# Gate projections beside attention: seven Strassen products for eight, their weights combined and split by other engines

## The chip, the cores and the metric

The kernel runs on one core of a Trainium2 chip. The metric is the device time of one execution in microseconds (us); three executions of the kernel before gave 3804.57, 3805.02 and 3805.33 us, so the median is 3805.02.

## The reference, cut to what matters

The program computes two transformer-like blocks one after the other, all in fp32 on 1024 tokens with 1024 features. The change touches the second block. It begins with one wide projection, whose last 4096 columns are four gates of 1024 features, and four mixers, of which the attention is one:

```python
h = rmsnorm_2(x, g_mix)
u = h @ w_in                                    # 28 blocks of 128 columns, then 32 blocks of gates
c_q, c_kv, k_r, u_pool, z, xbc, dt, lru_g, lru_x, gates = split(u)
y_a = mla_mixer(c_q, c_kv, k_r, ...)            # causal attention: 8 heads, 1024 queries
y_b, y_c, y_d = pool_mixer(...), ssd_mixer(...), rglru_mixer(...)
gates = sigmoid(gates.reshape(b, s, 4, 1024))
merged = gates[0] * (y_a @ w_branch[0]) + ... + gates[3] * (y_d @ w_branch[3])
```

## The kernel before, in words

Names in rows: `m_` are the tiles of this projection, `at_` those of attention, `sd_` those of the state-space mixer before it, `t_` and `b_` those of later stages (`b_high`, `b_rest` and `b2_high` also hold h here). PE is TensorE, ACT ScalarE, DVE VectorE, POOL GpSimd, SP SyncE. `ACTq` and `SPq` rows are DMA issues by that engine.

An fp32 product is made as three matmuls (`product3`, L98 to L102): every operand is split in a rounded high part and the low rest, and high by high (L100), high weight by low input (L101) and low weight by high input (L102) are summed in PSUM. Each of these takes 128 contracted rows, 128 weight columns and 512 tokens.

`Projection` makes the wide projection in units of 128 columns. The weights of a unit are 128x1024 (8 blocks of contraction): SP loads them (L2641, 512 KB), POOL rounds them (L2652) and forms the rest (L2654), PE multiplies them with h, 8 blocks by 3 matmuls for each of the two halves of 512 tokens, ACT copies each half out of PSUM (`take`, L2701), SP stores (L2707). Units 0 to 27 run beside the earlier mixers. The 32 gate units run inside `Attention`: they are what PE does while it waits for the softmax, in pieces of 24 matmuls before the loop (4, 3, 1 and 1 pieces) and in half pieces of 12 matmuls in it. The gates are 32 units x 2 halves x 24 = 1536 matmuls.

The order on each engine is written out by hand. `Attention` first reads its projections (ACT issues the loads, L3325 to L3331), takes the squares for two norms (L3341), makes values, queries and keys, and then loops over 64 steps n = 8h + b: head h, block b of 128 queries. In a step PE turns the probabilities of n (L3292), makes the scores of n+1 (L3254; at b = 7 the queries of the next head, L3235), does its half pieces (two for even b, one for odd b), and then multiplies probabilities and values of n (L3302). After b = 7 it does two half pieces more, then the first scores of the next head. DVE takes the maximum of the scores of n+1 (`greatest`, L3443 to L3450), and later scales the result of n (L3472). ACT copies the turned probabilities of n out of PSUM (L3384), then takes the exponential of n+1 (`weigh`, L3354, after the maximum), then copies gate halves (L2701). POOL only splits gate weights in this time, and SP only loads and stores for the gates. Engines wait for each other by semaphores and run their own list strictly in order.

## Time and profile before

| | |
|---|---|
| median of 3 runs | 3805.02 us |
| profiled execution, own time | 3803.0 us |
| its span | 3801.3 us |
| PE busy | 3474.2 us (91%) |
| DVE, ACT, POOL busy | 2420.9, 1581.9, 1122.8 us |
| mean granted TensorE clock | 0.957 |
| matmuls of the projection and gates (L100 m_b) | 960, 404.7 us |

A busy time is summed over one engine's instructions; the engines run beside each other. Idle time of an engine is given with what released it. Times within the span (2225.00, say) are us from its start.

### The profile page before, as it was taken

To read this page: it belongs to the slowest core of one execution; us is meant where nothing else is said; L and a number is where in the kernel's file an instruction comes from. 1 tells how busy PE (TensorE), PEld (TensorE's weight loads), DVE (VectorE), ACT (ScalarE), POOL (GpSimd) and SP (SyncE) were. 2 spreads that over 40 slices of the span, in tenths; PEclk is the share of its full clock that TensorE was granted. 3 is DMA by queue.
4 is the path that set the end of the run, shared out by engine and by line. 5 is a ranking of instruction groups with operands and counts; after the bars stand their busy time and mean duration, and the time that the engine had idled before them with its cause. 6 is when DMAs were issued, how large, how long until landed. Compare 5 with 4: busy or idle time off the path is not lost. (4 is left out here: it accounts for less than half of the span.)

```text
span 3801.3 us, 44335 instructions
## 1 busy us (share of the span) xinstructions
PE 3474.2 (91%) x16324; PEld 2772.5 (73%) x16324; DVE 2420.9 (64%) x2818; ACT 1581.9 (42%) x2197; POOL 1122.8 (30%) x673
## 2 busy tenths in 40 slices
PE   6899998596999999879989899999899889999997
PEld 3678777465888888756777667777677778878876
DVE  5569557747888888867655322222246488877778
ACT  4322234445777777735222222222232342234444
POOL 1232220145111111143321212222143455545543
PEclk9899999797999999989999999999999999999999
DMA  5312246647999999854421311111253524478854
GB/s 190 112 50 82 105 144 215 223 153 280 406 402 407 403 407 400 353 214 141 147 92 56 128 47 67 59 67 64 79 193 128 194 97 153 152 285 275 267 167 138
DMA packets 224984, 716.69 MB, mean 189 GB/s; under 512 B 26816, under 2 KB 61457, under 8 KB 208689
## 3 DMA queue, kind: packets, MB, share of 16 engines
q1 hardware_dynamic: 184000, 620.37, 45.0%
q10 hardware_dynamic: 31056, 64.28, 4.5%
q0 software_dynamic: 9760, 29.80, 2.0%
q8 instruction: 106, 1.74, 0.2%
q14 instruction: 62, 0.50, 0.0%
HBM read 573.47 MB, written 140.89 MB: 188 GB/s over the span
## 5 line engine op out<-in xcount | busy, mean ns | idle before, releaser
L100 PE MATMUL m_b<-b_high,m_high 128*128 128x512 f32 x960 | 404.7, 422 | 12.4 <-POOL m_low L2654 6.6
L102 PE MATMUL m_b<-b_high,m_low 128*128 128x512 f32 x960 | 377.3, 393 | 0.0
L101 PE MATMUL m_b<-b_rest,m_high 128*128 128x512 f32 x960 | 376.8, 393 | 0.0
L2652 POOL TENSOR_TENSOR m_high<-m_raw,m_one 128x1024 fp32r<-128x1024 f32 x60 | 119.2, 1986 | 761.3 <-PE m_b L102 684.0
L3948 POOL TENSOR_TENSOR t_wl<-t_buf,t_wh 128x512 fp32r<-128x512 f32 x136 | 195.2, 1441 | 240.6 <-ACT t_wh L4079 240.5
L100 PE MATMUL zs_z<-zs_hs,zs_high 128*128 128x512 f32 (+1 forms) x584 | 226.1, 387 | 8.5 <-DVE zs_hs L310 8.0
L2701 ACT ACTIVATE m_ob<-m_b 128x512 f32<-128x512 f32 x120 | 71.1, 596 | 376.3 <-PE m_b L102 341.1
L100 PEld LDWEIGHTS m_b<-b_high,m_high 128*128 128x128 f32 x960 | 182.7, 190 | 60.6 <-issue 12.4
L100 PE MATMUL t_b<-b_high,t_wh 128*128 128x512 f32 x544 | 215.4, 396 | 9.5 <-POOL t_wl L3948 9.5
L101 PE MATMUL zs_z<-zs_hs,zs_high 128*128 128x512 f32 (+1 forms) x584 | 218.7, 375 | 0.0
L102 PE MATMUL zs_z<-zs_hs,zs_low 128*128 128x512 f32 (+1 forms) x584 | 218.6, 374 | 0.0
L101 PEld LDWEIGHTS m_b<-b_rest,m_high 128*128 128x128 f32 x960 | 182.9, 190 | 45.9 <-issue 8.4
L101 PE MATMUL t_b<-b_rest,t_wh 128*128 128x512 f32 x544 | 213.7, 393 | 0.0
L102 PE MATMUL t_b<-b_high,t_wl 128*128 128x512 f32 x544 | 213.4, 392 | 0.0
L102 PEld LDWEIGHTS m_b<-b_high,m_low 128*128 128x128 f32 x960 | 182.0, 190 | 40.0
L2278 DVE TENSOR_TENSOR ex_wlo<-moe_raw,ex_who 128x2048 fp32r<-128x2048 f32 x78 | 178.7, 2292 | 50.4 <-ACT ex_who L2228 49.5
L2278 DVE TENSOR_TENSOR moe_mixl<-moe_late_rows,moe_mixh 128x2048 fp32r<-128x2048 f32 x78 | 178.8, 2293 | 42.4 <-ACT moe_mixh L2228 42.4
L4079 ACT ACTIVATE t_wh<-t_buf 128x512 fp32r<-128x512 f32 x136 | 85.8, 631 | 261.7 <-PE t_b L102 77.6
L2278 DVE TENSOR_TENSOR moe_mixl<-moe_raw,moe_mixh 128x2048 fp32r<-128x2048 f32 x80 | 182.5, 2283 | 5.3 <-PEq L48 5.3
L428 POOL TENSOR_TENSOR zs_high<-zs_raw,zs_one 128x1024 fp32r<-128x1024 f32 x29 | 59.0, 2035 | 411.8 <-PE zs_z L102 406.4
L3472 DVE TENSOR_SCALAR at_o<-m_b,at_sm 128x64 f32<-128x64 f32 x64 | 18.2, 284 | 230.2 <-PE m_b L3302 203.0
L2228 ACT ACTIVATE ex_who<-moe_raw 128x2048 fp32r<-128x2048 f32 x78 | 149.1, 1913 | 23.4 <-DMA moe_raw<-in_expert_w 18.2
(710 smaller groups left out, 9454.8 us busy)
## 6 DMA issues: line engine op xcount, KB each, us to landing
moe_raw<-in_expert_w SPq DMA_DIRECT2D x79, 2048.0 KB, 10.1
moe_late_rows<-in_expert_w SPq DMA_DIRECT2D x39, 2048.0 KB, 10.4
t_raw<-in_w_ff SPq DMA_DIRECT2D x192, 256.0 KB, 3.6
m_raw<-in_w_ug SPq DMA_DIRECT2D x60, 512.0 KB, 4.5
t_buf<-hid SPq DMA_DIRECT2D x112, 256.0 KB, 4.4
hid<-t_x SPq DMA_DIRECT2D x96, 256.0 KB, 2.3
yrows<-ex_y ACTq DMA_DIRECT2D x38, 512.0 KB, 11.4
gates<-m_ob SPq DMA_DIRECT2D x32, 512.0 KB, 2.9
```

The costliest lines, as they stand in the source:

```text
L100: nc.tensor.matmul(out, w[0], x[0], start=first, stop=False)
L101: nc.tensor.matmul(out, w[0], x[1], start=False, stop=False)
L102: return nc.tensor.matmul(out, w[1], x[0], start=False, stop=last)
L428: g.tensor_tensor(self.high[j][:], self.raw[j][:], self.one[:].broadcast_to([P, D]), ALU.mult).then_inc(self.rounded, 1)
L2228: S.activation(half(wh[u], x_), half(raw[slot], x_), ACT.Copy).then_inc(rounded, 1)
L2278: V.tensor_tensor(half(wl[u], x_), half(raw[slot], x_), half(wh[u], x_).bitcast(F32), ALU.subtract).then_inc(left, 1)
L2652: g.tensor_tensor(W.high[j][:], W.raw[j][:], W.one[:].broadcast_to([P, D]), ALU.mult).then_inc(W.rounded, 1)
L2701: self.nc.scalar.activation(self.ob[n % 2][:, c * BANK:(c + 1) * BANK], self.banks[m % len(self.banks)][:], ACT.Copy).then_inc(self.taken, 1)
L3472: V.tensor_scalar(self.o[p % 2][:, b, h % 2 * VH:(h % 2 + 1) * VH], ps[4][:, n % 2 * P:n % 2 * P + VH], sm[:, 1:2], None, ALU.mult).then_i ...
L3948: G.tensor_tensor(self.wl[:, f % 4], self.source(f), self.wh[:, f % 4].bitcast(F32), ALU.subtract).then_inc(self.split, 1)
L4079: S.activation(self.wh[:, f % 4], self.source(f), ACT.Copy).then_inc(self.rounded, 1)
```

## The change

The gates become a product of a 2 by 2 block matrix: the 1024 columns of contraction in two halves of 512, the 1024 tokens in two halves, and the 32 gate units as 16 pairs (units g and g + 16). For each pair Strassen's scheme (in the Winograd form) makes seven products of combined inputs instead of eight, each of 4 blocks of contraction by 3 matmuls. So there are 16 x 7 = 112 products f of 12 matmuls, 1344 in all. They run in seven phases of 16: ONE (f 0 to 15), TWO, THREE, SIX, SEVEN, FOUR, FIVE. Pieces before the loop become 8, 6, 2 and 2 products (216 matmuls, as many as the 4, 3, 1 and 1 pieces were); a step of the loop has one product, two at b = 4 and 6, and two more at a head's end: 12 for a head, where there were 14 half pieces.

What is new per product: SP loads 128x512 blocks of the weights (L2852) into seven places; where a product wants a sum of blocks, POOL makes it (`sum`, L2898); ACT rounds it (`high`, L2925, for up to three products ahead, LEAD); POOL forms the rest (`split`, L2911) in the order sum of product f+1, then the rest of f. One sum of three blocks per pair (`KEPT_SUM`, two POOL additions) is formed after product 13 + 3g//2, written to DRAM (`gate_sum`, L2816) and loaded again as one term of phases THREE and SIX. The products of ONE are copied out by ACT (L2960); the later ones are added by DVE (L2972) to partial results that SP stores and reads again (L2879, L2866); in phases SIX and FIVE DVE adds twice. The combined inputs of h for SIX, SEVEN, FOUR and FIVE are formed in place by DVE in 72 additions spread over the steps (`transform`, L2985 to L2997), and rounded by ACT (`round`, L3008). The combination of the seven products replaces no other work of the kernel; `take` for the gates is gone.

The diff, cut to its core; tables of places, the reads of partial results and the steps of `transform` are left out:

```diff
-        self.nc, self.R, self.h, self.total, self.banks = nc, R, h, 2 * N_UG, banks
-        self.W = Weights(nc, s, A["w_ug"], D, N_UG)
+        self.nc, self.R, self.h, self.total, self.banks = nc, R, h, 2 * N_U, banks
+        self.W = Weights(nc, s, A["w_ug"], D, N_U)
...
+class Gates:
+    PAIRS = 16
+    ONE, TWO, THREE, SIX, SEVEN, FOUR, FIVE = range(7)
+    KEPT = None
+    WEIGHTS = (((0, 0, 1),), ((0, 1, 1),), ((0, 1, 1), (KEPT, 0, -1)), ((KEPT, 0, 1),), ((0, 0, 1), (1, 0, -1)), ((1, 1, 1),), ((1, 0, 1), (1, 1, 1)))
+    KEPT_SUM = ((1, 0, 1), (1, 1, 1), (0, 0, -1))
...
+    RING, AHEAD, READ_AHEAD, LEAD = 4, 3, 2, 3
...
+        self.raw = [W.raw[0][:, lo], W.raw[0][:, hi], W.raw[1][:, lo], W.raw[1][:, hi], room[0], F.ob[1][:, lo], F.ob[1][:, hi]]
...
+        keep_after = {13 + 3 * g // 2: g for g in range(self.PAIRS)}
+        self.jobs = []
+        for f in range(self.total):
+            self.jobs.append(("product", f))
+            if f in keep_after:
...
+        self.sums_to, n = {}, 0
+        order = [("product", 0)]
+        for job in self.jobs:
+            order += [job] if job[0] == "keep" else [("product", job[1] + 1)] if job[1] + 1 < self.total else []
...
+    def keep_to(self, sp, g):
+        while self.kept_to <= g:
+            job = ("keep", self.kept_to)
+            sp.wait_ge(self.summed, self.sums_to[job])
+            sp.dma_start(self.R["gate_sum"][job[1]], self.raw[self.slot(job, 0)]).then_inc(self.kept, 16)
+            self.kept_to += 1
...
+    def weights(self, sp, job):
+        for i, (r, c, sign) in enumerate(self.terms[job]):
+            n = self.first_load[job] + i
+            slot = n % len(self.raw)
+            if n >= len(self.raw):
+                before, part = self.owner[n - len(self.raw)]
+                if part:
+                    sp.wait_ge(self.summed, self.sums_to[before] - len(self.terms[before]) + 1 + part)
+                elif before[0] == "keep":
+                    self.keep_to(sp, before[1])
+                    sp.wait_ge(self.kept, 16 * (before[1] + 1))
+                else:
+                    sp.wait_ge(self.split, before[1] + 1)
...
+            if r is self.KEPT:
+                g = job[1] % self.PAIRS
+                self.keep_to(sp, g)
+                sp.wait_ge(self.kept, 16 * (g + 1))
+                source = self.R["gate_sum"][g]
+            else:
+                source = self.A["w_ug"][N_U + job[1] % self.PAIRS + self.PAIRS * r][:, c * BANK:(c + 1) * BANK]
+            sp.dma_start(self.raw[slot], source).then_inc(self.w_in[slot], 16)
...
+    def store(self, sp, f):
+        x, g = divmod(f, self.PAIRS)
+        if x == self.ONE:
+            sp.wait_ge(self.copied, f + 1)
+        else:
+            sp.wait_ge(self.added, f - self.PAIRS + 1)
...
+    def step(self, sp, f):
+        self.weights_to(sp, f + self.AHEAD)
+        self.read(sp, f + self.READ_AHEAD)
+        self.store(sp, f)
...
+    def sum(self, pool, job):
+        terms = self.terms[job]
+        raw = self.raw[self.slot(job, 0)]
+        for i in range(1, len(terms)):
+            if i == 1:
+                self.landed(pool, job, 0)
+            self.landed(pool, job, i)
+            self.nc.gpsimd.tensor_tensor(raw, raw, self.raw[self.slot(job, i)], ALU.add if terms[i][2] > 0 else ALU.subtract).then_inc(self.summed, 1)
+            pool.wait_ge(self.summed, self.sums_to[job] - len(terms) + 1 + i)
+    def split_all(self, pool):
+        self.sum(pool, ("product", 0))
+        for job in self.jobs:
+            if job[0] == "keep":
+                self.sum(pool, job)
+                continue
+            f = job[1]
+            if f + 1 < self.total:
+                self.sum(pool, ("product", f + 1))
+            pool.wait_ge(self.high_made, f + 1)
+            self.nc.gpsimd.tensor_tensor(self.wl[f % self.RING], self.raw[self.slot(job, 0)], self.wh[f % self.RING].bitcast(F32), ALU.subtract).then_inc(self.split, 1)
+    def high(self, act, count):
+        for f in range(self.highs, min(count, self.total)):
+            job = ("product", f)
+            if len(self.terms[job]) > 1:
+                act.wait_ge(self.summed, self.sums_to[job])
+            else:
+                self.landed(act, job, 0)
+            if f >= self.RING:
+                act.wait_ge(self.used, f - self.RING + 1)
+            else:
+                act.wait_ge(self.F.W.used[f // 2], N_U // 2)
+            self.nc.scalar.activation(self.wh[f % self.RING], self.raw[self.slot(job, 0)], ACT.Copy).then_inc(self.high_made, 1)
+            self.highs += 1
...
+    def multiply(self, pe, count):
+        for f in range(self.made, min(self.made + count, self.total)):
+            x, j = f // self.PAIRS, f % self.RING
+            pe.wait_ge(self.split, f + 1)
...
+            for k in range(4):
+                for n in made:
+                    pe.wait_ge(self.t_low, n + k + 1)
+                part = slice(k * P, (k + 1) * P)
+                mm = product3(self.nc, self.bank(f), (self.wh[j][:, part], self.wl[j][:, part]), (high[k], low[k]), k == 0, k == 3)
+            mm.then_inc(self.used, 1)
+            self.made += 1
+    def copy(self, act, count):
...
+            act.wait_ge(self.used, f + 1)
+            self.nc.scalar.activation(self.part[slot], self.bank(f), ACT.Copy).then_inc(self.copied, 1)
+            self.out += 1
+            self.high(act, f + 1 + self.LEAD)
+    def add(self, dve, count):
+        for f in range(self.out, min(self.out + count, self.total)):
+            x = f // self.PAIRS
+            for slot, _, n in self.uses[f]:
+                dve.wait_ge(self.part_in[slot], 16 * (n + 1))
+            dve.wait_ge(self.used, f + 1)
+            for slot, _, _ in self.uses[f]:
+                ins = self.nc.vector.tensor_tensor(self.part[slot], self.part[slot], self.bank(f), ALU.subtract if x == self.FOUR else ALU.add)
+            ins.then_inc(self.added, 1)
+            self.out += 1
...
-        self.fills = [2 - b % 2 for b in range(self.QB)]
+        self.fills = [1 + (b in (4, 6)) for b in range(self.QB)]
...
     def tensor(self, pe):
-        F.multiply(pe, 4)
+        G.multiply(pe, 8)
...
-        F.multiply(pe, 3)
+        G.multiply(pe, 6)
...
-            F.halves(pe, self.fills[b])
+            G.multiply(pe, self.fills[b])
...
-                F.halves(pe, 2)
+                G.multiply(pe, 2)
...
     def scalar(self, act):
-        F.take(act, 4)
+        G.high(act, G.LEAD)
+        G.copy(act, 8)
...
+        made = 18
...
-            take(self.fills[b])
+            G.high(act, made + G.LEAD)
+            G.round(act, n)
+            made += self.fills[b] + 2 * last
             if last:
                 if h % 2:
                     pair(h // 2)
-                take(2)
...
     def vector(self, dve):
...
+            G.add(dve, self.fills[b])
+            G.transform(dve, n)
             dve.wait_ge(self.summed, n + 1)
...
+            if last:
+                G.add(dve, 2)
+        G.add(dve, G.total)
...
+                for f in range(G.total):
+                    G.step(sp, f)
+                G.over(sp)
...
-                for n in range(2, N_UG):
+                for n in range(2, N_U):
                     F.halve(pool_, n)
+                G.split_all(pool_)
```

Three places show how the instructions move. First ACT at the start of attention, with the issue of the last store of the state-space mixer (`sd_xo`). Before:

```order
L2701 ACTIVATE m_ob1<-m_b6 128x512
L3184 DMA y<-sd_xo 128x4x1024
L3331 DMA at_cq<-u 128x3x1024
...
L3331 DMA at_pT1<-in_w_uv 128x1024
L3325 DMA at_wq0<-in_w_uq 128x384
L3327 DMA at_wk0<-in_w_uk 128x256
L2701 ACTIVATE m_ob0<-m_b7 128x512
L2701 ACTIVATE m_ob0<-m_b5 128x512
L2701 ACTIVATE m_ob1<-m_b6 128x512
L2701 ACTIVATE m_ob1<-m_b7 128x512
L3341 ACTIVATE at_pT0<-at_cq 128x512 x3
```

The same place of the changed kernel:

```order
L2701 ACTIVATE m_ob1<-m_b6 128x512
L3482 DMA y<-sd_xo 128x4x1024
L3629 DMA at_cq<-u 128x3x1024
...
L3629 DMA at_pT1<-in_w_uv 128x1024
L3623 DMA at_wq0<-in_w_uq 128x384
L3625 DMA at_wk0<-in_w_uk 128x256
L2925 ACTIVATE m_high0<-m_raw0 128x512 x2
L2925 ACTIVATE m_high1<-m_raw1 128x512
L2960 ACTIVATE m_ob0<-m_b7 128x512
L2925 ACTIVATE m_high1<-m_raw1 128x512
L2960 ACTIVATE m_ob0<-m_b5 128x512
```

The rounding of the first gate weights, which POOL did by itself before, now stands on ACT behind the store and eight DMA issues.

Second, ACT at the turn from head 0 to head 1, the last copies of step 7 first (at_pr holds the exponentials, at_pT the turned probabilities). Before:

```order
L3384 ACTIVATE at_pT1<-m_b2 128x512
L3384 ACTIVATE at_pT1<-m_b3 128x512
L2701 ACTIVATE m_ob0<-m_b7 128x512
...
L2701 ACTIVATE m_ob1<-m_b5 128x512
L3354 ACTIVATE at_pr0,at_sm0<-m_b0,at_mx0 128x128
L3325 DMA at_wq1<-in_w_uq 128x384
L3384 ACTIVATE at_pT0<-m_b2 128x128
L3354 ACTIVATE at_pr1,at_sm1<-m_b0,at_mx1 128x256
L2701 ACTIVATE m_ob1<-m_b6 128x512
```

The same place of the changed kernel; the three rounds after the second exponential are those of products 30, 31 and 32:

```order
L3676 ACTIVATE at_pT1<-m_b2 128x512
L3676 ACTIVATE at_pT1<-m_b3 128x512
L2925 ACTIVATE m_high0<-m_raw1 128x512
L2925 ACTIVATE m_high0<-m_ob1 128x512
L3008 ACTIVATE b2_high<-at_t 128x512
L3653 ACTIVATE at_pr0,at_sm0<-m_b0,at_mx0 128x128
...
L3676 ACTIVATE at_pT0<-m_b2 128x128
L3653 ACTIVATE at_pr1,at_sm1<-m_b0,at_mx1 128x256
L2925 ACTIVATE m_high1<-m_raw1 128x512
L2925 ACTIVATE m_high1<-at_groom0 128x512
L2925 ACTIVATE m_high0<-m_raw0 128x512
```

In the changed kernel product 30, which PE has next after the scores of block 1, is rounded behind the exponential of these scores; before, ACT had nothing there that the pieces of PE wait for.

Third, SP where the gates begin; from there to the end of attention it goes on in this alternation. Before:

```order
L2707 DMA u<-m_ob0 128x1024
L2641 DMA m_raw1<-in_w_ug 128x1024
L2707 DMA u<-m_ob1 128x1024
L2641 DMA m_raw0<-in_w_ug 128x1024
L2707 DMA gates<-m_ob0 128x1024
L2641 DMA m_raw1<-in_w_ug 128x1024
L2707 DMA gates<-m_ob1 128x1024
```

In the changed kernel SP has this where kept sums and products of two terms meet (head 1, products 32 and 33; the weight and partial loads and the stores of results alternate with writes of kept sums):

```order
L2852 DMA m_ob1<-in_w_ug 128x512 x2
L2816 DMA gate_sum<-m_raw0 128x512
L2852 DMA m_raw0<-in_w_ug 128x512 x2
L2852 DMA m_raw1<-gate_sum 128x512
L2866 DMA at_kr<-gate_part 128x512
L2879 DMA gates<-at_groom1 128x512
L2852 DMA m_raw1<-in_w_ug 128x512
L2852 DMA at_groom0<-in_w_ug 128x512
L2816 DMA gate_sum<-m_ob1 128x512
L2852 DMA m_ob1<-in_w_ug 128x512 x2
L2852 DMA m_raw0<-gate_sum 128x512
```

And POOL there, from the sum of product 32 to the rest of product 32:

```order
L2898 TENSOR_TENSOR m_raw0<-m_raw0,m_raw1 128x512
L2911 TENSOR_TENSOR m_low1<-at_groom0,m_high1 128x512
L2898 TENSOR_TENSOR m_ob1<-m_ob1 128x512
L2898 TENSOR_TENSOR m_ob1<-m_ob1,m_raw0 128x512 x2
L2911 TENSOR_TENSOR m_low0<-m_raw0,m_high0 128x512
```

The places of the seven blocks come round after two or three products, so that a load of SP stands behind the write of a kept sum, and the rest of a product stands on POOL behind the sum of the next one and a kept sum.

## Rows read from the trace of the kernel before

**Rows 1.** Busy time, stretch by stretch: attention's loop.
```profile
core 0: us, PE busy (x) PEld busy (x) DVE busy (x) ACT busy (x) POOL busy (x), PEclk, DMA share, GB/s
2225.00:2745.00 520.00, 505.13 (x2501) 396.17 (x2499) 129.76 (x435) 138.70 (x346) 110.94 (x52) 1.00 0.18 61
```

**Rows 2.** Waits in the same stretch: engine, line, releaser; us, times, longest.
```profile
POOL m_high L2652 <- PE m_b L102: 379.1, 26, 21.2
ACT m_ob L2701 <- PE m_b L102: 150.0, 39, 7.3
PE m_b L3292 <- ACT at_pr L3354: 9.8, 7, 1.4
```

**Rows 3.** Timeline of PE and ACT, start of attention: start, us, instruction, idle before.
```profile
2124.83 0.39 PE L100 MATMUL m_b<-b_high,m_high 128*128 128x512 f32 x1
...
2125.04 0.38 ACTq L3184 DMA_DIRECT2D y<-sd_xo  x1
...
2134.14 0.37 ACTq L3331 DMA_DIRECT2D at_cq<-u  x1
...
2138.38 1.09 ACT L2701 ACTIVATE m_ob<-m_b 128x512 f32<-128x512 f32 x2 [12.76 <-issue]
...
2146.36 0.39 PE L102 MATMUL m_b<-b_high,m_low 128*128 128x512 f32 x1
...
2148.48 1.15 ACT L3341 ACTIVATE at_pT<-at_cq 128x512 f32<-128x512 f32 x2 [1.09 <-DMA at_pT<-in_w_uv]
```

**Rows 4.** The page's costliest groups: ACT rounding 128x512 in a later stage.
```profile
L4079 ACT ACTIVATE t_wh<-t_buf 128x512 fp32r<-128x512 f32 x136 | 85.8, 631 | 261.7 <-PE t_b L102 77.6
```

**Rows 5.** POOL forming rests, by tile: ns least/median/most, first and last start.
```profile
L3948 POOL TENSOR_TENSOR t_wl<-t_raw,t_wh x90: 1268/1295/1770, 3032.3 to 3634.3; 128x512 fp32r<-128x512 f32 x90
L2654 POOL TENSOR_TENSOR m_low<-m_raw,m_high x60: 2338/2390/3442, 1641.1 to 2703.0; 128x1024 fp32r<-128x1024 f32 x60
```

**Rows 6.** Timeline of PE where it had waited, and a stretch there (columns as rows 1).
```profile
2220.17 0.33 PE L3292 MATMUL m_b<-all_ident,at_pr 128*128 128x128 f32 x1 [2.23 <-ACT at_pr L3354]
...
2220.58 0.97 PE L100 MATMUL m_b<-b_high,m_high 128*128 128x512 f32 x1
...
2227.64 0.39 PE L102 MATMUL m_b<-b_high,m_low 128*128 128x512 f32 x1
```
```profile
2221.00:2223.00 2.00, 2.00 (x6) 1.58 (x5) 0.95 (x4) 0.57 (x2) 0.00 (x0) 0.50 0.00 0
```

**Rows 7.** Timeline at the start of a head.
```profile
2355.18 0.33 PE L3292 MATMUL m_b<-all_ident,at_pr 128*128 128x128 f32 x1 [1.40 <-ACT at_pr L3354]
2355.35 0.60 PE L3254 MATMUL m_b<-at_k,at_q 128*128 128x256 f32 x2
...
2355.59 0.58 PE L100 MATMUL m_b<-b_high,m_high 128*128 128x512 f32 x1
2355.98 0.30 DVE L3443 TENSOR_TENSOR m_b<-m_b,all_cutq 128x128 f32<-128x128 f32 x1 [1.35 <-PE m_b L3254]
...
2356.77 0.15 DVE L3450 TENSOR_SCALAR at_mx<-at_mx 128x1 f32<-128x1 f32 x1
...
2356.96 0.48 ACT L3354 ACTIVATE at_pr<-m_b,at_mx 128x256 f32<-128x256 f32 x1 [1.14 <-DVE at_mx L3450]
...
2357.34 0.19 ACT L3354 ACTIVATION_READ_ACCUMULATOR at_pr<-m_b,at_mx 128x1 f32 x1
...
2361.04 0.39 PE L102 MATMUL m_b<-b_high,m_low 128*128 128x512 f32 x1
```

**Rows 8.** VectorE's groups by line and shape: busy, mean ns, idle before.
```profile
L4360 DVE TENSOR_TENSOR b_rest<-t_buf,b_high 128x512 fp32r<-128x512 f32 x64 | 77.7, 1226 | 23.8 <-ACT b_high L4122 23.1
L4369 DVE TENSOR_TENSOR t_x<-t_x,t_b 128x512 f32<-128x512 f32 x48 | 32.9, 685 | 6.5 <-PE t_b L102 4.3
```

**Rows 9.** The page's DMA issues: KB each, median us from issue to landing.
```profile
t_raw<-in_w_ff SPq DMA_DIRECT2D x192, 256.0 KB, 3.6
...
hid<-t_x SPq DMA_DIRECT2D x96, 256.0 KB, 2.3
```

**Rows 10.** Timeline of SP's issue, and of PE four steps on in the same head.
```profile
2362.01 0.69 PE L100 MATMUL m_b<-b_high,m_high 128*128 128x512 f32 x1
...
2362.45 0.43 SPq L2641 DMA_DIRECT2D m_raw<-in_w_ug  x1
...
2388.12 0.69 PE L100 MATMUL m_b<-b_high,m_high 128*128 128x512 f32 x1
```

More of the change, by code:

```diff
@@ L3219, in tensor @@
     def tensor(self, pe):
-        mm_, ps, C, turn, F = self.nc.tensor.matmul, self.ps, self.C, self.nc.tensor.transpose, self.F
-        F.multiply(pe, 4)
+        mm_, ps, C, turn, G = self.nc.tensor.matmul, self.ps, self.C, self.nc.tensor.transpose, self.gates
+        G.multiply(pe, 8)
         for c in range(2):
@@ L3344, in scalar @@
             S.activation(self.rs[w][:], self.rs[w][:], ACT.Sqrt).then_inc(self.rooted, 1)
-        F.take(act, 3)
+        G.copy(act, 6)
         for c in range(self.QB):
@@ L3365, in pair @@
             act.dma_start(self.R["y"][p], self.yT[:]).then_inc(self.stored, 16)
-        F.take(act, 2)
+        G.copy(act, 2)
         weigh(0)
         weights(1)
-        begun, made = 0, F.moved
-        def take(parts):
-            nonlocal begun
-            begun += parts
-            F.take(act, made + begun // 2 - F.moved)
+        made = 18
         for n in range(MH * self.QB):
@@ L3476, in vector @@
                 greatest(n + 1)
+            if last:
+                G.add(dve, 2)
+        G.add(dve, G.total)
     def over(self, eng):
@@ L3497, in mixers @@
             att = Attention(nc, s, q, A, R, F, banks, C, rope, (ssd,))
+            G = att.gates = Gates(nc, s, q, A, R, F, att, ssd)
         with nc.Block() as block:
@@ L3509, in _ @@
                 lru.constants(sp)
-                for n in range(N_UG):
+                for n in range(N_U):
                     if n >= 2:
@@ L3519, in _ @@
                     ssd.load(sp, n)
-                for n in range(N_UG - 2, N_UG):
+                    if n == N_U - 2:
+                        G.weights_to(sp, G.AHEAD - 1)
+                for n in range(N_U - 2, N_U):
                     F.landed(sp, n)
+                for f in range(G.total):
+                    G.step(sp, f)
+                G.over(sp)
                 att.over(sp)
@@ L3547, in _ @@
                 att.scalar(act)
-                F.take(act, N_UG * 2)
             @block.vector
```

162 lines of the change are left out of this document (151 added, 11 removed).

## The prediction

> **What bounds the kernel now.** I read first the stretch by stretch view of attention's loop, then the waits of that stretch, then the timelines of its start and of one head. In the loop PE is busy for 505.13 of 520.00 us at a granted clock of 1.00, while DVE, ACT and POOL have 129.76, 138.70 and 110.94 us [rows 1]. The waits say the same: POOL waits 379.1 us and ACT 150.0 us for PE's matmuls, and PE's only wait of size is 9.8 us, seven times at a head's start, for the first exponential of a head [rows 2]. So in this stretch every matmul left out is time gained, and every wait that PE is given is time lost. What hides the gates' other work is that it is done a whole unit ahead of PE.
>
> **A. The matmuls that go.** 1536 become 1344, so 192 go. From 2124.83 to 2146.36 PE starts 96 in a row, 95 distances in 21.53 us, 0.2266 us each [rows 3]. 192 x 0.2266 = 43.5 us gained, all on the path, since PE has nothing else to wait for there. The matmuls before the loop stay 216, so this is all gained in the loop.
>
> **B. The start of attention.** Before, the weights of the first gate unit are split by POOL, which has nothing else to do, and PE goes on at 2124.83. After, the first rounding is on ACT, behind the store of the state-space output and eight DMA issues. ACT issues that store at 2125.04, issues the next DMA only when it has landed, at 2134.14, and is free at 2138.38 [rows 3]. Then come one rounding, for which the nearest row is 0.631 us [rows 4], and one rest, 1.295 us [rows 5], with the hops between: PE starts product 0 at about 2140.4, 15.6 us late. Before, ACT was held just as long, but only copies of PSUM stood there, and three banks took PE's pieces meanwhile. The squares, which start at 2148.48, are the next thing on the path and move with PE, since they stand behind the copy of product 7 now, and ACT rounds product 10 first (0.6 and a copy, 1.5 in all). PE is also idle long enough to lose its clock. After an idle time of 2.23 us the granted clock was 0.50 in the next 2 us, which is the lower level, 1.2 GHz, and the 24 matmuls behind it took 7.06 us from the first start to the last end's start [rows 6], against 5.45 us for the same 24 in the middle of the loop, from 2355.59 to 2361.04 [rows 7]: 1.6 us. B is 15.6 + 1.6 + 1.5 = 19 us, between 13 (the time that ACT is held, 2125.04 to 2138.38) and 22.
>
> **C. The start of heads 1 to 7.** ACT rounds for three products ahead, but counts the two products of a head's end only after them, so at b = 7 it has rounded just to the end of the head. The first product of the new head is rounded behind the exponential of block 1. PE reaches that product right after the scores of block 1, and waits for the maximum (2355.98 to 2356.92, 0.94 us), the exponential with its read-out (2356.96 to 2357.53, 0.57) [rows 7], the rounding (0.63) and the rest (1.30): 3.4, with hops 3.7 us. In the row the pieces simply start at 2355.59, while DVE and ACT do this. Nothing else covers it: PE's next work, probabilities by values, stands behind the product. Does the clock fall for 3.7 us? The rows show both: 2.23 us of idle lost it and 1.6 us [rows 6], and the usual 1.40 us at a head's start did not, as the clock over the loop is 1.00 [rows 1, 7]. 3.7 lies beyond the one that lost it, and I take the loss. So 7 x (3.7 + 1.6) = 37.1, and at the two heads where DVE's double additions (0.685 each [rows 8], two more of them) stand ahead of the maximum 2 x 1.4 = 2.8: 39.9 us. The bounds are 7 x 3.4 = 24, without a loss of clock, and 47, with one more addition at each head.
>
> The Trainium skill, page "TensorE: Matmul & The Clock Gate", section "HAM oscillation — how this bites in real kernels", has a rule that speaks against the change: work on TensorE that is short between two waits starts cold after each wait, so the price is paid at every one of them. By it the sum has C at 39.9; by the 1.40 us row alone C would be 28.7 and the time 3842. The trace agrees with the rule for 2.23 us of idle and not for 1.40.
>
> **D. Kept sums among products of two terms (products 31 to 36).** Seven places hold the weight blocks. From product 31 to 36 each product wants two blocks, and four kept sums want three each, so a block is loaded when the job two back lets go of it, and that job is often a kept sum that must be added, written and read first. Per step of the long kind: two POOL sums of 128x512 (half of a 128x1024 operation of 2.39 us, 1.2 each [rows 5]) 2.4; write of the kept sum 2.3 [rows 9]; two or three issues on SP's queue, of which one is 0.43 [rows 10], 1.1; landing of 256 KB 3.6 [rows 9]; sum 1.2 and rest 1.3 [rows 5]: 11.7 us with one rest at the end. A short step, with the kept sum already out, has issue, landing, sum and rest, 6.5 us. I read the order of the queues as long, short, short, long, short: 43 us. PE goes through the five products in 23.4 us: four steps from 2362.01 to 2388.12 [rows 10] are 26.1 us, less one half piece of 2.7. The chain is 19.5 us longer. To that I add 3 us since the rest of product 31 stands on POOL behind the sum of 32, whose loads stand on SP behind a store of a result that DVE adds only after the new head's first maximum, and two cold starts, 3.2. D is 26 us. This is the least sure term: if the loads run ahead by three products as they do elsewhere it is 0, and if every step is long (5 x 11.7 - 23.4 and the rest) 45.
>
> **E. The start of the loop.** The loads of products 20 and 21 stand on SP behind the store of product 16, and DVE adds that only after the first maximum; ACT blocks in `high` meanwhile. PE's lead there is two products, so a few us come out: 4, between 0 and 8.
>
> **F. VectorE.** DVE takes on 96 products of one or two additions (128 x 0.685 = 88 us [rows 8]) and 72 transforms, for which the nearest row is a subtraction of two 128x512 SBUF operands, 1.226 us [rows 8]: 88 us. With its 130 it has some 306 of about 480 us. The additions stand behind exponential and sum in each step, with a product (2.7 us) of cover before the maximum of the step after next; where a transform piece and two products fall together the maximum is late. 3 us, between 0 and 10. ACT takes on some 107 roundings of 0.63 and gives up 55 copies; POOL has 94 rests and 80 sums of about 1.25 us, 218 us in place of 111, and DMA some 496 transfers of 256 KB, about 260 GB/s in place of 61: all have room on average [rows 1], and I cost them at nothing beyond B to E. What covers them is PE's 5.1 us per product (480 by 94); if that cover were gone, POOL would cost 2.3 us a product.
>
> **Sum.** -43.5 + 19 + 39.9 + 26 + 4 + 3 = +48.4 us on the profiled execution's 3803.0, so 3851.4. The median of the runs lies 2.0 above that execution (3805.02), so I forecast 3853 us. By the lower bounds it is -43.5 + 13 + 24 = -6.5 us, 3798; by the upper ones -43.5 + 22 + 47 + 45 + 8 + 10 = +88.5, 3893.
>
> **The rivals.**
> 1. *The chain of kept sums never reaches PE* (not slower). The loads of 31 to 36 run far enough ahead, since POOL and DMA idle on average, and the clock survives waits of 3.7 us. Then D, E and F are 0, C is its lower 24, B 19: -0.5 us, 3804. For it: 379 us of idle POOL [rows 2]. Against it: the seven places and SP's strict order leave no way to run ahead. It decides once PE's lead over the rests stays above one product through product 36. A step on is its other half: if in addition PE's start is covered, because B's 13 us of waiting were ACT's alone and something of attention could move up, it is -43.5 + 24 = -19.5, 3785. Against that: PE's list has nothing between the first product and the squares.
> The Trainium skill has a rule that backs this rival, on the page "DMA: Bandwidth & Descriptors", section "Rules for kernel authors": issued early and waited for late, a transfer's fixed cost lies beside the computing. By that rule D would be 0. No row of this trace shows a load held by a reused place as short as these.
> 2. *DVE and POOL hold each other up* (slower still). 72 transforms and 174 operations of POOL work on SBUF in the same time. If each transform waited for one operation of POOL, 72 x 1.3 = 94 us would come on DVE, of which about half is beyond its free time in the steps where they fall: +45, 3898. For it: rests on POOL take up to 1.77 us where the median is 1.295 [rows 5]. Against it: that the median is so near the least, 1.268, with DVE at work in the same stretch.
> The Trainium skill, page "SBUF — State Buffer", section "SBUF: two separate sides", says that VectorE and GpSimd share a pair of ports and that an operation with two SBUF inputs locks the other out for its whole length. The medians do not show it as a rule for every operation.
> 3. *PE is not the bound*, so that the matmuls left out bring nothing. 505 of 520 us busy [rows 1] excludes it.
>
> **How the numbers follow.** A run can tell 0.2% from no change, 7.6 us here: below 3797.4 is faster, above 3812.6 slower. The forecast, slower by 0.2% to 2.3%, has 0.72; rival 2 0.06; rival 1 0.12 without and 0.10 with its second half. So faster 0.10, same 0.12, slower 0.78. The range is 3797 to 3893, the two sums of bounds rounded out, with 0.16 outside.
>
> **What would show it.** A: 192 fewer matmuls of L100 to L102 on m_b. B: PE idle for 15 us before the first product of attention, released by POOL's rest, and ACT's first rounding right behind its DMA issues. C: seven waits of PE for POOL's rest of over 3 us at the starts of heads 1 to 7, and clock 0.50 behind them. D: waits of PE for the rest of products 32 to 36 in head 1 of together some 20 us, with POOL waiting for DMA. F: waits of PE for exponentials longer than 1.4 us. The prediction is wrong if PE has no such wait at the heads, if those in D sum to under 5 us, or if waits for DVE or for partial results, which I cost at nothing, are the largest.

## The result, and the profile after

The changed kernel took 3876.03 us in the median of four runs, 1.0192 of the kernel before (interval 1.018 to 1.0205), some 71 us more. The forecast was 3853 with a range to 3893, so sign and main mechanism held and the size came out a third too small. The profiled execution has a span of 3875.2 us, 73.9 more than before, and the whole difference lies in the stretch of attention, from the first gate product that PE could take (2124.83 before, 2126.28 after) to the end of attention's last matmul (2740.36 and 2815.68): 615.5 us became 689.4. The stretch, and below it the loop, of before and then of after (columns as in [rows 1]):

```profile
2124.83:2740.36 615.53, 596.40 (x2809) 455.64 (x2807) 163.72 (x466) 159.16 (x380) 132.35 (x62) 0.99 0.20 69
2220.17:2740.36 520.19, 509.96 (x2514) 400.04 (x2514) 130.71 (x439) 138.46 (x347) 110.94 (x52) 1.00 0.18 61
```
```profile
2126.28:2815.68 689.40, 586.91 (x2616) 438.52 (x2616) 316.57 (x666) 200.95 (x460) 254.08 (x192) 0.93 0.59 202
2241.15:2815.68 574.53, 497.19 (x2322) 380.96 (x2322) 279.60 (x639) 164.83 (x401) 216.51 (x165) 0.93 0.62 208
```

The second numbers carry the account. PE has 2809 - 2616 = 193 operations fewer on record (192 by the program), worth 43.5 us at the forecast's price, but its busy time fell by only 9.5 us: what was left ran 34.0 us longer, at a mean granted clock of 0.93 in place of 0.99. And PE's idle time rose from 19.1 to 102.5 us, 83.4 more. -9.5 + 83.4 = 73.9. What PE waited for in the stretch (us, times, longest):

```profile
PE m_b L100 <- POOL m_low L2911: 69.9, 16, 14.5
PE m_b L3590 <- ACT at_pr L3653: 16.4, 16, 1.4
PE m_b L3539 <- DVE at_ckv L3703: 6.0, 1, 6.0
PE m_b L3600 <- ACT at_pT L3676: 5.6, 2, 4.9
```

Before, there was no wait of the first kind, and the second was this over the whole loop ([rows 2] begins after the first of the eight):

```profile
PE m_b L3292 <- ACT at_pr L3354: 12.0, 8, 2.2
```

So the 16.4 us are eight more waits, none longer than 1.4. The largest of the first kind, in the changed kernel, in order of time (start, us of the matmul, and in brackets the wait before it): one before the loop, five in head 1, and one at the start of each later head, those of heads 4 and 5 left out here:

```profile
2140.74 0.80 PE L100 MATMUL m_b<-b_high,m_high 128*128 128x512 f32 x1 [14.46 <-POOL m_low L2911]
...
2321.53 0.80 PE L100 MATMUL m_b<-b_high,m_high 128*128 128x512 f32 x1 [5.15 <-POOL m_low L2911]
2331.82 0.50 PE L100 MATMUL m_b<-b_high,m_high 128*128 128x512 f32 x1 [4.33 <-POOL m_low L2911]
2344.92 0.79 PE L100 MATMUL m_b<-b_high,m_high 128*128 128x512 f32 x1 [6.90 <-POOL m_low L2911]
2360.99 0.80 PE L100 MATMUL m_b<-b_high,m_high 128*128 128x512 f32 x1 [3.33 <-POOL m_low L2911]
2373.97 0.80 PE L100 MATMUL m_b<-b_high,m_high 128*128 128x512 f32 x1 [7.50 <-POOL m_low L2911]
2421.55 0.80 PE L100 MATMUL m_b<-b_high,m_high 128*128 128x512 f32 x1 [3.70 <-POOL m_low L2911]
2490.16 0.79 PE L100 MATMUL m_b<-b_high,m_high 128*128 128x512 f32 x1 [4.49 <-POOL m_low L2911]
...
2698.20 0.80 PE L100 MATMUL m_b<-b_high,m_high 128*128 128x512 f32 x1 [3.50 <-POOL m_low L2911]
2763.45 0.79 PE L100 MATMUL m_b<-b_high,m_high 128*128 128x512 f32 x1 [4.55 <-POOL m_low L2911]
```

The start of head 6 shows the chain of term C, and answers to [rows 7]: maximum, exponential, then the rounding, then the rest, and PE's first product of the head only behind it.

```profile
2694.10 0.60 PE L3552 MATMUL m_b<-at_k,at_q 128*128 128x256 f32 x2
...
2695.53 0.15 DVE L3743 TENSOR_SCALAR at_mx<-at_mx 128x1 f32<-128x1 f32 x1
...
2695.72 0.47 ACT L3653 ACTIVATE at_pr<-m_b,at_mx 128x256 f32<-128x256 f32 x1 [1.14 <-DVE at_mx L3743]
...
2696.18 1.14 ACT L2925 ACTIVATE m_high<-m_raw 128x512 fp32r<-128x512 f32 x2
2696.88 2.49 POOL L2911 TENSOR_TENSOR m_low<-m_raw,m_high 128x512 fp32r<-128x512 f32 x2 [20.27 <-ACT m_high L2925]
```

POOL's idle time of 20.27 us before its rest, and ACT's rounding without a wait of its own right behind the exponential, say that nothing but ACT's place in line was late.

Head by head, from the first turn of a head to that of the next (the last to the end of the stretch), in us; "start" is what lies ahead of head 0:

| | start | 0 | 1 | 2 | 3 | 4 | 5 | 6 | 7 |
|---|---|---|---|---|---|---|---|---|---|
| before | 95.3 | 66.2 | 68.8 | 64.6 | 68.8 | 64.5 | 68.8 | 64.6 | 53.8 |
| before less 24 matmuls (5.4) | 95.3 | 60.7 | 63.4 | 59.1 | 63.4 | 59.1 | 63.4 | 59.1 | 48.4 |
| after | 114.9 | 74.5 | 101.5 | 67.8 | 72.8 | 67.4 | 68.8 | 64.2 | 57.6 |
| lost against line 2 | 19.5 | 13.7 | 38.1 | 8.7 | 9.4 | 8.2 | 5.4 | 5.0 | 9.2 |

### The profile page after: what moved, and what is told of

Same layout as the page of the kernel before. It is cut to its first block and busy times, and to the rows that moved or that the text cites. A ratio compares the mean times of both kernels' runs of the same rounds, so it can differ in the third digit from the quotient of the medians.

```text
span 3875.2 us, 45336 instructions
## 1 busy us (share of the span) xinstructions
PE 3468.5 (90%) x16132; PEld 2758.7 (71%) x16132; DVE 2572.0 (66%) x3018; ACT 1623.8 (42%) x2277; POOL 1235.2 (32%) x801
## 5 line engine op out<-in xcount | busy, mean ns | idle before, releaser
L100 PE MATMUL m_b<-b_high,m_high 128*128 128x512 f32 x896 | 390.0, 435 | 82.3 <-POOL m_low L2911 69.9
L102 PE MATMUL m_b<-b_high,m_low 128*128 128x512 f32 x896 | 362.0, 404 | 0.0
L101 PE MATMUL m_b<-b_rest,m_high 128*128 128x512 f32 x896 | 361.7, 404 | 0.0
L2278 DVE TENSOR_TENSOR ex_wlo<-moe_raw,ex_who 128x2048 fp32r<-128x2048 f32 x78 | 178.7, 2292 | 50.4 <-ACT ex_who L2228 49.7
L2228 ACT ACTIVATE moe_mixh<-moe_raw 128x2048 fp32r<-128x2048 f32 x76 | 145.7, 1918 | 25.4 <-PE ex_pu L102 24.0
L2652 POOL TENSOR_TENSOR m_high<-m_raw,m_one 128x1024 fp32r<-128x1024 f32 x28 | 58.7, 2098 | 289.7 <-PE m_b L102 221.6
L4253 POOL TENSOR_TENSOR t_wl<-t_raw,t_wh 128x512 fp32r<-128x512 f32 x90 | 121.8, 1362 | 86.1 <-ACT t_wh L4384 85.9
```

The lines of the kernel that those rows point to most:

```text
L100: nc.tensor.matmul(out, w[0], x[0], start=first, stop=False)
L101: nc.tensor.matmul(out, w[0], x[1], start=False, stop=False)
L102: return nc.tensor.matmul(out, w[1], x[0], start=False, stop=last)
L2228: S.activation(half(wh[u], x_), half(raw[slot], x_), ACT.Copy).then_inc(rounded, 1)
L2278: V.tensor_tensor(half(wl[u], x_), half(raw[slot], x_), half(wh[u], x_).bitcast(F32), ALU.subtract).then_inc(left, 1)
L2652: g.tensor_tensor(W.high[j][:], W.raw[j][:], W.one[:].broadcast_to([P, D]), ALU.mult).then_inc(W.rounded, 1)
```

## The experiments

Ratios are to the kernel before, measured beside each experiment, with their 95% interval; a stretch is that of attention in the profiled execution, as above (689.4 us in the changed kernel).

**1. The first product of a head rounded before the head's first exponential.**

```diff
                 if h + 1 < MH:
+                    G.high(act, made + 1)
                     weigh(n + 1)
```

> The changed kernel, but at a head's end ACT rounds the first product of the next head before the exponential of that head, not behind the second one. My theory (PE waits at the starts of heads 1 to 7 because that rounding stands behind the exponential): the seven waits for POOL's rest, 28.5 us together in the changed kernel's trace, go, and the clock that PE loses behind each (about 1.5 us) with them; head 1 gives some of it back since the kept sums are late there anyway. So 3876 less 30 to 39: about 3842. Rival (the rounding is only one of two late things, the loads or the sums behind it are as late): the waits stay with another releaser, and the time is over 3862.

Measured: 1.0164 (1.0147 to 1.018), 3861.39 us, some 11 us less than the changed kernel's ratio makes, with runs from 3852.95 to 3869.17; the profiled one is the fastest of them, with a stretch of 670.3, 19.1 less. By the ratio, a third of my 30 to 39 us came, and the heads of the fastest run say why. Heads 3, 5 and 6 went from 72.8, 68.8 and 64.2 to 66.3, 63.4 and 59.1, that is 6.5, 5.4 and 5.1 less, and their clock was 1.00. Heads 2, 4 and 7 stayed at 68.0, 66.9 and 56.4: there the wait moved to the second product (4.24, 4.84 and 2.84 us). Head 1 gave 2.1 us, the kept sums holding it as before. POOL makes the sum of the next product ahead of the rest of this one, so a second product waits where the third is a sum of two blocks. That is so in heads 2, 4 and 7, in phases THREE, SEVEN and FIVE; head 5 begins with the last two sums of SEVEN, but its third product, like those of heads 3 and 6, wants one block. So the theory holds where the third product wants one block, and the rival where it wants two. In head 2 of this run the store of a result stands on SP (2410.97) behind DVE's additions, which come after the new head's first maximum; only then SP issues the load of a kept sum for product 44, and POOL's sum waits 9.54 us for it, ahead of the rest of 43:

```profile
2409.81 0.15 DVE L3744 TENSOR_SCALAR at_mx<-at_mx 128x1 f32<-128x1 f32 x1
...
2410.26 0.69 DVE L2972 TENSOR_TENSOR m_sin<-m_sin,m_b 128x512 f32<-128x512 f32 x1 [0.30 <-issue]
...
2410.97 0.32 SPq L2879 DMA_DIRECT2D gate_part<-m_sin  x1
...
2412.04 0.40 SPq L2852 DMA_DIRECT2D m_raw<-gate_sum  x1
...
2416.62 1.26 POOL L2898 TENSOR_TENSOR m_ob<-m_ob,m_raw 128x512 f32<-128x512 f32 x1 [9.54 <-DMA m_raw<-gate_sum]
```

**2. The first products rounded before ACT waits for the store.**

```diff
         S, ps, F, G = self.nc.scalar, self.ps, self.F, self.gates
+        G.high(act, G.LEAD)
+        G.copy(act, 1)
         for e in self.earlier:
             e.over(act)
...
-        G.high(act, G.LEAD)
-        G.copy(act, 8)
+        G.copy(act, 7)
```

> The changed kernel, but ACT rounds the first three products and copies the first result out before it waits for the state-space store and issues attention's loads. My theory (PE's 14.5 us of waiting before product 0 come from that place on ACT): PE works through products 0 to 3 in that time and waits some 2 us before product 4, so 10 to 13 us less, about 3864. Rival (the next stage waits for loads that land as late as before, so that PE waits the same before the squares): under 4 us less, over 3872.

Measured: 1.0197 (1.018 to 1.0214), 3875.90 us, no change. The rival held, as to its kind: PE's wait of 14.46 us became waits of 2.55, 1.87, 1.85 and 3.79, and the first sums of squares came only 1 us earlier. The next thing was the loads: that of product 5 stands on SP behind the store of product 1, which waits for ACT's copy, which stands behind the eight DMA issues. ACT then waited 7.28 us for it:

```profile
2138.45 0.60 ACT L2960 ACTIVATE m_ob<-m_b 128x512 f32<-128x512 f32 x1 [3.75 <-issue]
...
2139.07 0.33 SPq L2879 DMA_DIRECT2D gate_part<-m_ob  x1
2139.45 0.43 SPq L2852 DMA_DIRECT2D m_ob<-in_w_ug  x1
...
2147.33 0.63 ACT L2925 ACTIVATE m_high<-m_ob 128x512 fp32r<-128x512 f32 x1 [7.28 <-DMA m_ob<-in_w_ug]
```

**3. No kept sums.**

```diff
-        keep_after = {13 + 3 * g // 2: g for g in range(self.PAIRS)}
+        keep_after = {}
...
-    WEIGHTS = (..., ((0, 1, 1), (KEPT, 0, -1)), ((KEPT, 0, 1),), ...
+    WEIGHTS = (..., ((0, 1, 1), (0, 0, -1)), ((0, 0, 1),), ...
```

> The changed kernel without the kept sums: no three loads, two additions, write and reload for a pair; phases THREE and SIX take one plain block in the place of the kept sum, so two of the three terms of that sum are left out of the result. Loads, sums of two terms, partial results and transforms stay. My theory (the waits of PE for the rests of products 31 to 36, 22 us and some 8 us of clock, and those of head 0, some 10 us, come from the kept sums' loads and writes in the seven places): 30 to 42 us less, about 3840, and no wait over 2 us in heads 0 and 1 but that at the head's start. Rival (products of two terms alone, or the partial results, hold the chain): the waits of head 1 stay at over half, and the time is over 3860.

Measured: 1.007 (1.0053 to 1.0087), 3829.69 us, some 46 less, more than the 30 to 42 of my theory; stretch 644.3. Head 0 went from 74.5 to 59.8, head 1 from 101.5 to 71.6, the others by less than 2 us. All that head 0 had lost is the kept sums' (59.8 against 60.7 in line 2 of the table), and 29.9 us of head 1. The waits at the heads' starts stayed, 3.50 in head 1 to 4.56 in head 7.

**4. The kernel before with fewer matmuls.**

```diff
+        cut = part is not None and ms[0] % 5 == 0
-        for k in range(KD) if part is None else range(part * KD // 2, (part + 1) * KD // 2):
+        for k in (... as before ...) if not cut else (part * (KD - 1),):
```

> The kernel before, with 198 of the gates' 1536 matmuls left out inside the loop (18 of 24 in every fifth piece, 11 pieces; their products are left out of the result); loads, splits, copies and stores stay. My theory (PE is the bound in the loop, 0.2266 us a matmul): 44.9 us less, about 3760. Rival (other engines or the softmax chain come out as soon as PE has less to do): half of that or less, over 3782.

Measured: 0.9906 (0.9889 to 0.9922), 3766.55 us, 35 us less, 0.18 a matmul where I had 0.2266. PE is the bound, but not alone: where a cut piece stood, the exponential was late. These waits rose from the eight of 12.0 us to

```profile
PE m_b L3293 <- ACT at_pr L3355: 19.2, 14, 2.6
```

This experiment cut 9 of the 12 matmuls of a half piece, often both halves of a piece in one step, more unevenly than the change does; heads 5 and 6 of experiment 1 show the full 5.4 us.

**5. The kept sums at other places.**

```diff
-        keep_after = {13 + 3 * g // 2: g for g in range(self.PAIRS)}
+        keep_after = {11: (0, 1, 2), 17: tuple(range(3, 9)), **{19 + 2 * i: (9 + i,) for i in range(7)}}
...
-        self.weights_to(sp, f + self.AHEAD)
+        self.weights_to(sp, f + (5 if f in (7, 13) else self.AHEAD))
```

> The changed kernel with the kept sums at other places: three after product 11 and six after product 17, where PE does norms, keys and values, and the other seven after products 19, 21 to 31, one for two products, none after 31; SP's loads run two products further ahead at these two places. Leaving the sums out altogether took 45 us off the stretch. My theory (the cost lies in where the sums stand: four of them among the products of two terms, and 1.5 products apart in heads 0 and 1): 25 to 40 us less than the changed kernel, about 3843, and no wait over 2 us between the starts of heads 1 and 2 but the one at the start. Rival (seven places are too few for the sums wherever they stand, so the waits only move into the time before the loop): under 12 us less, over 3862.

Measured: 1.0177 (1.016 to 1.0194), 3873.05 us, some 6 us less by the ratio, within the two intervals. The rival held: head 1 got shorter, from 101.5 to 77.5, but in its place came a wait of 6.42 before product 12 and one of 19.92 at the first turn of head 0. The sums put after product 17 could not begin there, since ACT rounds 17 only after the values; they ran from 2232.91 on, and ACT stood 25.89 us in the rounding of a product whose block is loaded behind theirs, with the first exponential in its queue.

**6. The second with the loads of products 0 to 6 ahead of the first store.**

```diff
+                G.weights_to(sp, 6)
                 for f in range(G.total):
                     G.step(sp, f)
```

> The changed kernel with the early rounding of the second experiment, and SP issues the loads of products 0 to 6 before its first store of a result. The early rounding alone gave nothing, as products 5 and 6 then waited for their loads, which stand on SP behind a store that waits for ACT's copy. My theory (two holds in a row: ACT's place, and SP's order): 8 to 12 us less than the changed kernel, about 3866. Rival (the third thing, ACT's eight DMA issues, which hold the copies and the roundings of the next products till 2138, is as late): under 4 us less, over 3871.

Measured: 1.0182 (1.0165 to 1.0199), 3872.84 us, some 3 us less, within the two intervals: by the time, the rival's outcome. In the profiled run, the fastest of the four, the stretch is 683.6, 5.8 less, and the wait of 3.79 before product 5 is gone, so the loads were one hold. Two more are seen in its trace, and no run takes them apart: product 4, whose rounding stands right behind ACT's eight issues (PE waits 2.54), and ACT's waits for a store to land (4.11) and for the next loads (2.49, 1.92 and 2.16) ahead of the squares, for which PE waits 4.05.

**7. All repairs at once,** with one of DVE's two additions at a head's end ahead of the first maximum:

```diff
+                G.add(dve, 1)
                 greatest(n + 1)
+                G.add(dve, 1)
-            if last:
+            elif last:
                 G.add(dve, 2)
```

> The changed kernel with the repairs of the head's start, of the attention's start and of the kept sums together, and one of the two additions at a head's end ahead of the first maximum. Sum of the parts by my theory: start of heads 19 as measured plus what the kept sums hid of it (10), kept sums 30, start 10: 69 us less than the changed kernel's 3876, about 3807, level with the kernel before. Rival (the products of two terms hold the heads' starts and the chain through the loads as well): 25 us or more stay, about 3832.

Measured: 1.0046 (1.0029 to 1.0063), 3824.16 us, between the two. The new wait of experiment 5 is in it (20.26 us before head 0), and still the heads 2 to 6 came to 61.7, 66.0, 60.2, 63.4 and 59.4: the earlier addition, with the earlier rounding, took the wait from the heads with two blocks too. Neither the rounding alone (experiment 1) nor the other places alone (experiment 5: 68.2 and 68.1) shortened heads 2 and 4; the earlier addition alone was not run.

**8. No transforms.**

```diff
-        for x in range(16):
+        for x in range(0):
...
-            made = [4 * i for i, t in enumerate(self.T) if t[0] == x and f % self.PAIRS == 0]
+            made = []
```

> The changed kernel with the 72 additions on h and their 16 roundings left out (phases SIX to FIVE multiply with plain blocks of h, so the results are not the gates). My theory (DVE has room; they cost PE some late maxima only): 3 to 8 us less, about 3870. Rival (DVE and POOL hold each other up on SBUF, or DVE's list is what makes maxima late at most steps): over 20 us less, under 3856.

Measured: 1.0164 (1.0147 to 1.0181), some 10 us less, stretch 680.3: 9.1 less, a little over what I expected of my theory and far from the rival. PE's waits for exponentials fell from 16.4 us (16) to 11.4 (9), which is the late maxima; the other 4 us were not followed.

**9 and 10. The repairs with the kept sums placed by what experiment 5 showed.**

```diff
-        keep_after = {11: (0, 1, 2), 17: tuple(range(3, 9)), **{19 + 2 * i: (9 + i,) for i in range(7)}}
+        keep_after = {10: (0, 1), 16: tuple(range(2, 8)), **{18 + 7 * i // 4: (8 + i,) for i in range(8)}}       # 9
+        keep_after = {10: (0,), 16: tuple(range(1, 6)), **{17 + 3 * i // 2: (6 + i,) for i in range(10)}}        # 10
```

> All repairs of the seventh experiment, with the kept sums placed by what its trace showed: its sums after product 17 began only at 2225, since the rest of 17 stands behind ACT's rounding of 17, which comes after the values, and so held the first exponential 20 us; those after 11 held product 11 for 6 us. Now two after product 10, six after 16 (whose rest is formed before the values), and eight from 18 to 30. My theory (the wait before the loop is the sums' chain holding ACT's rounding of products 20 and 21): 20 to 28 us less than the seventh's 3824, about 3799, within 0.2% of the kernel before. Rival (the sums cost the same wherever they stand, as their loads come through the same seven places): under 8 us less, over 3816.

> The same with one kept sum after product 10, five after 16 and ten from 17 to 30, 1.5 products apart as in the changed kernel. Theory: fewer sums before the loop, so no wait there, but the waits of head 0 (4.9 us, and some of 1 to 2) stay: within 5 us of the run before it, about 3801. Rival (as there): over 3816.

In both, SP's loads run one product further ahead at the two places where experiments 5 and 7 had two.

Measured: experiment 9 0.9988 (0.9979 to 0.9998), 3799.82 us, as forecast: it beats the kernel before by 0.12%, with an interval that ends just short of none. Experiment 10, 1.0017 (1.0008 to 1.0026), 3809.56, missed: I had it within 5 us of experiment 9, and with ten sums in the loop in place of eight it took some 10 us more. Its profile, of one of its slowest runs (3816.40), has a wait of 8.87 us before the second product of head 1, where experiment 9 has 5.02. Experiments 3, 5, 9 and 10 together say that the price of a kept sum is mostly that of its place. In the profile of experiment 9, the stretch and PE's first waits in it:

```profile
2124.20:2735.58 611.38, 566.48 (x2617) 423.24 (x2616) 323.01 (x666) 200.44 (x460) 254.63 (x192) 0.98 0.68 228
```
```profile
PE m_b L100 <- POOL m_low L2910: 19.1, 11, 5.0
PE m_b L3589 <- ACT at_pr L3653: 16.6, 16, 1.4
```

611.4 us against 615.5 before, with the changed kernel's waits for exponentials and 19.1 us in place of 69.9 for rests. The start takes 105.7 us, still 10 more than before, and head 1 keeps that one wait. Against line 2 of the table the stretch still loses 39 us: 10.4 at the start, 9.1 and 7.2 in heads 0 and 1, 5.4 in head 7 and 7 in the others together. So nearly all that the missing matmuls are worth is still spent.

## Why the prediction was right, and where its sizes were off

**What bounds, and A.** Right. With the wait at its start gone, heads 5 and 6 of experiment 9 take 63.4 and 59.3 us, where 24 matmuls fewer by the forecast's 0.2266 us make 63.4 and 59.1. These are its two best heads; in the others something else still costs 1 to 9 us.

**B.** Right in size: 19.5 us by the table, against 19. Its cause was told too simply. The forecast named one hold, ACT's place behind the store and the issues; experiment 2 shows another behind it, SP's loads, which wait for ACT's copies, so that taking away the first alone gave nothing. With the loads moved too (experiment 6), only some 6 us of the profiled stretch came back, and what each of the holds seen there costs stays open.

**C.** Right. The seven waits are 5.15, 3.70, 4.49, 3.56, 3.56, 3.50 and 4.55, together 28.5 us; the forecast's waits were 7 x 3.7 + 2.8 = 28.7, and of heads 2 to 7 the two with the double additions (heads 3 and 7, 4.49 and 4.55) are the ones that stand out. That the sums agree so well is in part luck: head 1's 5.15 has 1.65 of the kept sums in it (3.50 without them, experiment 3). The forecast's upper bound of 47 is not what its words make: one more addition at each head gives 39.9 + 7 x 0.685 = 44.7, which would take some 2 us off the upper end of its range. The clock falls behind the seven waits, as the forecast chose; ahead of the start of head 6, and behind its wait of 3.50 (columns as in [rows 1]):

```profile
2686.00:2693.00 7.00, 6.54 (x34) 5.39 (x32) 1.77 (x4) 1.09 (x2) 0.00 (x0) 1.00 0.18 75
2698.50:2700.50 2.00, 2.00 (x6) 1.52 (x6) 0.00 (x0) 0.63 (x1) 1.51 (x2) 0.50 0.92 304
```

Wait and clock together were 5.4 and 5.1 us in heads 5 and 6 and 6.5 in head 3 (experiment 1), against 5.3 and 6.7 forecast. The rule on the clock that the forecast weighed, from the Trainium skill's page "TensorE: Matmul & The Clock Gate", section "HAM oscillation — how this bites in real kernels", held here for waits of 3.5 us; the heads of experiment 1 with no wait over 0.9 us but the usual 1.40 kept a clock of 1.00. Between the two the length of a wait alone does not tell: behind the 2.55 us before product 0 of experiment 2 the clock stayed at 1.00, and behind 2.07 us in head 0 of experiment 1 (before 2274.86) it was 0.50, so the forecast's step from 2.23 us to 3.7 was a choice that came out, not a rule that the rows give:

```profile
2125.80:2134.00 8.20, 8.20 (x36) 6.65 (x36) 0.91 (x1) 0.60 (x1) 2.41 (x2) 1.00 0.82 307
```
```profile
2275.30:2277.30 2.00, 2.00 (x7) 1.52 (x6) 1.90 (x6) 0.00 (x0) 0.00 (x0) 0.50 0.93 358
```

**D.** Right in place and chain, and somewhat short in size. The rests of products 31 and 36 end the two sides of it: 2330.51 to 2378.72 is 48.2 us for five steps, against 43 forecast. The rests of 32 to 36 begin 13.1, 6.7, 9.3, 13.0 and 6.1 us after the one ahead, where the forecast had long, short, short, long, short at 11.7 and 6.5 (its own terms for a long step add to 11.9). PE's waits at products 31, 32, 34 and 35 are 22.1 us together, where it had some 20. (Product 31 itself, the last of phase TWO, wants one block; the forecast's words have two.) In both long steps POOL waits nearly 8 us for the load of a term. SP issues it (2337.30) behind two other loads (2336.40), and the first of these goes into a place that is free only when a newer kept sum has been added there and written out (2334.39):

```profile
2330.51 1.26 POOL L2911 TENSOR_TENSOR m_low<-at_groom,m_high 128x512 fp32r<-128x512 f32 x1
...
2334.39 0.33 SPq L2816 DMA_DIRECT2D gate_sum<-m_ob  x1
...
2336.40 0.81 SPq L2852 DMA_DIRECT2D m_ob<-in_w_ug  x2
2337.30 0.38 SPq L2852 DMA_DIRECT2D m_raw<-gate_sum  x1
...
2342.26 1.26 POOL L2898 TENSOR_TENSOR m_ob<-m_ob,m_raw 128x512 f32<-128x512 f32 x1 [7.89 <-DMA m_raw<-gate_sum]
...
2343.60 1.26 POOL L2911 TENSOR_TENSOR m_low<-m_raw,m_high 128x512 fp32r<-128x512 f32 x1
...
2372.66 1.26 POOL L2911 TENSOR_TENSOR m_low<-m_ob,m_high 128x512 fp32r<-128x512 f32 x1
...
2378.72 1.27 POOL L2911 TENSOR_TENSOR m_low<-at_groom,m_high 128x512 fp32r<-128x512 f32 x1
```

Left out, the kept sums gave back 29.9 us in head 1; forecast 26.

**E.** This is the term that was mis-sized most. I had "a few us", 4, with 8 as the upper bound, from the loads of products 20 and 21 behind the store of 16. Head 0 lost 13.7 us, and experiment 3 gives all of it to the kept sums. I had looked for their chain only among products of two blocks; in head 0 two of three products are followed by one, which makes three loads a product on average through the same seven places, and ACT, standing in `high` for a load (8.39 us), held the turned probabilities, and through them PE for 4.88 us, the longest wait of this head:

```profile
2252.41 0.63 ACT L2925 ACTIVATE m_high<-m_raw 128x512 fp32r<-128x512 f32 x1 [8.39 <-DMA m_raw<-in_w_ug]
2252.95 0.37 ACT L3676 ACTIVATE at_pT<-m_b 128x256 f32<-128x256 f32 x1
...
2253.37 1.11 PE L3600 MATMUL m_b<-at_v,at_pT 128*128 128x64 f32 x4 [4.88 <-ACT at_pT L3676]
```

**F.** 3 us forecast, 9 to 10 measured (experiment 8), at its upper bound. Its sign, waits for exponentials longer than 1.4 us, did not come: there are more of them, and none is longer. The sum of the three differences, 10 in E, 4 in D and 6 in F, makes up for nearly all of the 48 us forecast against 71 measured.

**The rivals.** The first, that the kept sums' chain never reaches PE and that the clock survives, fell with D and C. The second, DVE against POOL, is there in the rows and small on the path (below). The third was excluded as said, and experiment 4 agrees, with 35 of 45 us.

## What to carry to other kernels

An engine that takes over a step for another brings its whole list with it: look up what stands ahead of the step on the new engine at each turn of the loop, and whether what is asked for next waits behind the softmax. A lead that is counted in steps is no lead where the count stops short of a turn; and with few buffers in a ring, a helper job of three loads is cheap only where the bound engine has something else to do. Arithmetic saved (43.5 us) is easily outspent by waits of 3.5 us, each of which here also cost the clock.

## What the runs showed of the hardware

A VectorE addition of two SBUF operands takes 0.69 us by itself and up to 1.77 us beside POOL: in the rows of this case that lie so, it ends 0.55 us after the POOL operation within which it began. It goes both ways: a rest on POOL that begins within such an addition takes up to 1.81 us in place of 1.27. The 128 additions of L2972, with one operand in PSUM, all take 0.68 to 0.69. From the changed kernel's timeline:

```profile
2506.05 0.68 DVE L2994 TENSOR_TENSOR at_t<-b_high,b_rest 128x512 f32<-128x512 f32 x1
2506.15 1.72 POOL L2911 TENSOR_TENSOR m_low<-m_raw,m_high 128x512 fp32r<-128x512 f32 x1 [3.87 <-ACT m_high L2925]
...
2512.02 1.35 POOL L2911 TENSOR_TENSOR m_low<-at_groom,m_high 128x512 fp32r<-128x512 f32 x1 [4.15 <-ACT m_high L2925]
2512.16 1.76 DVE L2997 TENSOR_TENSOR at_t<-at_t,b_rest 128x512 f32<-128x512 f32 x1
```

The Trainium skill, page "SBUF — State Buffer", section "SBUF: two separate sides", says that VectorE and GpSimd share a pair of ports, and that whichever of a VectorE operation with two SBUF inputs and a GpSimd operation that reads SBUF starts first holds it for its whole instruction. The rows agree. Over the 72 transforms it is 68.7 us in place of 72 x 0.69 = 49.7, so 19 us of DVE; all that the transforms cost the path is 10 us at most (experiment 8). My price for a transform from the nearest row, 1.226 us [rows 8], had this contention already in it: the 64 operations behind that mean take from 0.675 to 1.785 us.
